# An expert gets 112 slots in place of 128, and the overflow pass three blocks in place of two

## The reference

```
s    = sigmoid(h @ router_w);  sb = s + router_b            # 16 experts in 4 groups
grp  = group with the largest sum of its two best sb
eidx = the two best experts inside grp;  w = s[eidx] / sum(s[eidx])
for e in 16 experts:
    a = silu(h @ w_g[e]) * (h @ w_u[e])                       # 1024 -> 512
    y = y + gates[:, e] * (a @ w_d[e])                        # 512 -> 1024
x = x + gate2 * y
```

## Time and profile before

| | |
|---|---|
| timed runs, us | 1648.64, 1649.46, 1653.35 |
| profiled execution, from first to last instruction | 1646.0 us (3.5 under the median; the profile gives no other time of its own) |
| TensorE busy, multiplications | 1567.6 us, 95%, 7693 |
| VectorE, ScalarE, GpSimd busy | 64%, 56%, 32% |
| moved by DMA | 381.8 MB, mean 232 GB/s |
| granted TensorE clock, mean | 0.984 |

### The profile page before, as it was taken

The page is one execution under the profiler, slowest core; times in us unless marked ns, Lnnn a source line. Parts: engine busy times, 40 slices in busy tenths (PEclk is TensorE's granted clock), DMA queues, the critical chain, the costliest instruction groups (busy, mean ns, idle before and its releaser), DMA issues.

```text
span 1646.0 us, 21287 instructions
## 1 busy us (share of the span) xinstructions
PE 1567.6 (95%) x7693; PEld 1234.8 (75%) x7693; DVE 1047.2 (64%) x1385; ACT 923.8 (56%) x1284; POOL 530.5 (32%) x271
## 2 busy tenths in 40 slices
PE   7999999989999999999889999999999989999996
PEld 4677778877775887888676777787767778888885
DVE  2226546673355898998862357377433479899998
ACT  3343445434335788888644343444353458888893
POOL 2344554444532111111234445444445131111112
PEclk9999999999998999999999999999999999999998
DMA  9765343344359999999946543422443469999995
GB/s 363 265 199 167 115 128 91 102 130 143 115 174 334 344 385 362 370 377 364 368 170 210 187 154 112 133 90 89 144 147 111 157 224 379 378 368 378 381 368 205
DMA packets 153822, 381.77 MB, mean 232 GB/s; under 512 B 21060, under 2 KB 26886, under 8 KB 153724
## 3 DMA queue, kind: packets, MB, share of 16 engines
q1 hardware_dynamic: 122704, 325.32, 56.2%
q10 hardware_dynamic: 20140, 36.56, 6.3%
q0 software_dynamic: 10880, 18.59, 3.1%
HBM read 378.55 MB, written 27.93 MB: 247 GB/s over the span
## 4 chain that ended last, share of the span: by engine, by line
PE 70%; DVE 12%; DMA 10%; ACT 5%; issue 2%; ACTq 0%; SPq 0%; POOL 0%; DVEq 0%; POOLq 0%
PE ps L606 56%; PE ps L615 4%; DVE wxl L2466 4%; DMA raw<-w_e_down 4%; DMA raw<-w_e_up 3%; PE ps L639 2%; PE ps L952 2%; ACT wxh L1826 1%; DMA own<-w_mod 1%; PE ps L980 1%; PE ps L886 1%; DVE uv L2241 1%; ACT wh L1331 1%; PE ps L658 1%; PE ps L650 1%
## 5 line engine op out<-in xcount | busy, mean ns | idle before, releaser
L1949 POOL TENSOR_TENSOR wl<-raw,wh 128x1024 fp32r<-128x1024 f32 x168 | 409.8, 2443 | 531.7 <-ACT wh L1331 531.5
L2466 DVE TENSOR_TENSOR wxl<-raw,wxh 128x1024 fp32r<-128x1024 f32 x384 | 454.5, 1220 | 55.2 <-ACT wxh L1826 52.5
L1826 ACT ACTIVATE wxh<-raw 128x1024 fp32r<-128x1024 f32 x384 | 402.6, 1061 | 92.4 <-DMA raw<-w_e_down 35.4
L606 PE MATMUL ps<-wxh,xeT 128*128 128x512 f32 x1024 | 341.3, 399 | 4.0 <-issue 2.5
L1331 ACT ACTIVATE wh<-raw 128x1024 fp32r<-128x1024 f32 x168 | 176.7, 1056 | 227.6 <-PE ps L606 223.2
L606 PE MATMUL ps<-wh,hTh 128*128 128x512 f32 x720 | 293.2, 407 | 5.9 <-DVE hTl L2088 3.3
L606 PE MATMUL ps<-wh,hTl 128*128 128x512 f32 x720 | 281.9, 392 | 0.0
L606 PE MATMUL ps<-wl,hTh 128*128 128x512 f32 x720 | 281.5, 391 | 0.0
L606 PEld LDWEIGHTS ps<-wxh,xeT 128*128 128x128 f32 x1024 | 193.3, 189 | 46.8 <-issue 4.3
L606 PE MATMUL ps<-wxl,xeT 128*128 128x512 f32 x512 | 199.9, 390 | 0.0
L606 PEld LDWEIGHTS ps<-wh,hTh 128*128 128x128 f32 x720 | 135.7, 188 | 40.7 <-issue 7.9
(11 more groups left out here) (282 smaller groups left out, 2177.3 us busy)
## 6 DMA issues: line engine op xcount, KB each, us to landing
raw<-w_e_gate SPq DMA_DIRECT2D x128, 512.0 KB, 6.5
raw<-w_e_up SPq DMA_DIRECT2D x128, 512.0 KB, 5.8
raw<-w_e_down SPq DMA_DIRECT2D x128, 512.0 KB, 5.5
raw<-w_in SPq DMA_DIRECT2D x120, 512.0 KB, 3.7
own<-w_mod ACTq DMA_DIRECT2D x27, 1024.0 KB, 7.6
raw<-w_mod SPq DMA_DIRECT2D x36, 512.0 KB, 5.1
raw<-w_br_b SPq DMA_DIRECT2D x16, 512.0 KB, 3.8
raw<-w_out SPq DMA_DIRECT2D x16, 512.0 KB, 3.8
```

What stands on the lines that cost most here:

```text
L606: ins = pe.matmul(out, act_hl[i], w_hl[j], start=start and n == 0, stop=stop and n == 2)
L1826: act.activation(wxh[:, q % RING_MOE, :, :], raw[:, place, :, :], ACT.Copy).then_inc(sem("hi_done"), 1)
L1949: pool.tensor_tensor(wl[:, p % RING, :, :], raw[:, PAIR_CHUNK[p] % RAW, :, :], wh[:, p % RING, :, :].bitcast(F32), ALU.subtract).then_inc( ...
L2466: dve.tensor_tensor(wxl[:, q % RING_MOE, :, :], raw[:, expert_chunk(l, 0, q)[0], :, :], wxh[:, q % RING_MOE, :, :].bitcast(F32), ALU.subtr ...
```

## The change

The number of slots per expert becomes `SLOTS = 112`. All tiles keep their size; each instruction that handles an expert's slots takes 112 of the 128 partitions (where slots lie on partitions) or 112 of each 128 columns (where they lie in the free dimension). The overflow pass starts at rank 112 and has three blocks of 128 ranks in place of two, so its body is longer by a third block on every engine. Outside that body the instructions of each engine and their order are the same as before.

```diff
+SLOTS = 112
+BLOCKS_OVER = -(-(T - SLOTS) // P)
 def second_pass(eng, l, turn):
-                for b in (1, 2):
+                for b in range(1, BLOCKS_OVER + 1):
                     turn(e, b)
...
 # tensor_program
 def turn_rows(k, half, bank):
-    last = transpose(ps[:, bank, i * P:(i + 1) * P], xg[:, k % 2, first:first + 2 * P - 1:2])
+    last = transpose(ps[:, bank, i * P:i * P + SLOTS], xg[0:SLOTS, k % 2, first:first + 2 * P - 1:2])
 def up_pair(e, q, k, i):
-    last = mm3(ps[:, 2 + i // 4, :], (xeT[:, k % 2, 0, j, :], xeT[:, k % 2, 1, j, :]),
+    last = mm3(ps[0:SLOTS, 2 + i // 4, :], (xeT[:, k % 2, 0, j, 0:SLOTS], xeT[:, k % 2, 1, j, 0:SLOTS]),
 def down_pair(e, q, i):
-    last = mm3(ps[:, bank, :], (src[:, 0, j, :], src[:, 1, j, :]),
+    last = mm3(ps[0:SLOTS, bank, :], (src[:, 0, j, 0:SLOTS], src[:, 1, j, 0:SLOTS]),
 def turn_act(count):
-    last = transpose(ps[:, 0, j * P:(j + 1) * P], ae[:, j * P:(j + 1) * P])
+    last = transpose(ps[:, 0, j * P:j * P + SLOTS], ae[0:SLOTS, j * P:(j + 1) * P])
...
 # scalar_program
 def gate_part(count, pair):
-    act.activation(sg[:, :], ps[:, 2, :], ACT.Silu)
+    act.activation(sg[0:SLOTS, :], ps[0:SLOTS, 2, :], ACT.Silu)
 def rows_hi(count, k):
-    act.activation(xeT[:, k % 2, 0, :, :], ps[:, 0:2, :].rearrange("p b (k n) -> p (b k) n", n=P), ACT.Copy
+    act.activation(xeT[:, k % 2, 0, :, 0:SLOTS], ps[:, 0:2, :].rearrange("p b (k n) -> p (b k) n", n=P)[:, :, 0:SLOTS], ACT.Copy
...
 # gpsimd_program
-    pool.indirect_dma_start(xg[:, k % 2, :], None, h2_rows[:, :],
+    pool.indirect_dma_start(xg[0:SLOTS, k % 2, :], None, h2_rows[:, :],
...
 # vector_program
-dve.tensor_scalar(flag[:, 0:1], cnt[:, 0:1], float(P - SLOT_BASE), None, ALU.is_gt)
+dve.tensor_scalar(flag[:, 0:1], cnt[:, 0:1], float(SLOTS - SLOT_BASE), None, ALU.is_gt)
 def rows_lo(e, k, count):
-    dve.tensor_tensor(xeT[:, k % 2, 1, :, :], ps[:, 0:2, :].rearrange("p b (k n) -> p (b k) n", n=P),
-                      xeT[:, k % 2, 0, :, :].bitcast(F32), ALU.subtract)
+    dve.tensor_tensor(xeT[:, k % 2, 1, :, 0:SLOTS], ps[:, 0:2, :].rearrange("p b (k n) -> p (b k) n", n=P)[:, :, 0:SLOTS],
+                      xeT[:, k % 2, 0, :, 0:SLOTS].bitcast(F32), ALU.subtract)
 def turn(e, b):
-    dve.tensor_scalar(cnt[:, 2:5], slot[...], float(-P * b), None, ALU.add)
+    dve.tensor_scalar(cnt[:, 2:5], slot[...], float(-(SLOTS + P * (b - 1))), None, ALU.add)
```

More of the change, by code:

```diff
@@ L1158, in token_sums @@
                 for t in range(NT):
-                    last = pe.matmul(out, pick[:, k % 2, t, :], tokens_r[:, t, :], start=t == 0, stop=t == NT - 1)
+                    last = pe.matmul(out, pick[:, k % 2, t, 0:SLOTS], tokens_r[:, t, :], start=t == 0, stop=t == NT - 1)
                 last.then_inc(sem("idx_acc"), 1)
@@ L1315, in tensor_program @@
                     for s in range(2):
-                        last = pe.matmul(ps[:, LAST_BANKS[u], :], pickT[:, odd, t, :], oes[odd][:, s, half * W:(half + 1) * W],
+                        last = pe.matmul(ps[:, LAST_BANKS[u], :], pickT[0:SLOTS, odd, t, :], oes[odd][0:SLOTS, s, half * W:(half + 1) * W],
                                          start=odd == 0 and s == 0, stop=odd == 1 and s == 1)
@@ L1843, in act_hi @@
                 act.wait_ge(sem("eT_acc"), at("eT_acc", l, 1) + count)
-                act.activation(dst[:, 0, :, :], ps[:, 0, :].rearrange("p (k n) -> p k n", k=4), ACT.Copy
+                act.activation(dst[:, 0, :, 0:SLOTS], ps[:, 0, :].rearrange("p (k n) -> p k n", k=4)[:, :, 0:SLOTS], ACT.Copy
                                ).then_inc(sem("eT_hi"), 1)
@@ L1852, in out_row @@
                     act.wait_ge(sem(name), (e - k % 2) * 8 + at(name, l, 0))
-                act.activation(oe_rows[k % 2][:, :].rearrange("p (b n) -> p b n", b=2), ps[:, 4:6, :], ACT.Identity,
-                               scale=slot_gate[:, k % 4:k % 4 + 1]).then_inc(sem("out_hi"), 1)
+                act.activation(oe_rows[k % 2][0:SLOTS, :].rearrange("p (b n) -> p b n", b=2), ps[0:SLOTS, 4:6, :], ACT.Identity,
+                               scale=slot_gate[0:SLOTS, k % 4:k % 4 + 1]).then_inc(sem("out_hi"), 1)
             def out_hi(k, pair):
@@ L1859, in out_hi @@
                 act.wait_ge(sem("scattered0"), at("scattered0", l, 16 * LOOSE // 2))
-                act.activation(oes[k % 2][:, 0, :].rearrange("p (b n) -> p b n", b=2), ps[:, 4:6, :], ACT.Identity,
-                               scale=slot_gate[:, k % 4:k % 4 + 1]).then_inc(sem("out_hi"), 1)
+                act.activation(oes[k % 2][0:SLOTS, 0, :].rearrange("p (b n) -> p b n", b=2), ps[0:SLOTS, 4:6, :], ACT.Identity,
+                               scale=slot_gate[0:SLOTS, k % 4:k % 4 + 1]).then_inc(sem("out_hi"), 1)
             def expert(e, k):
@@ L1889, in scalar_program @@
                 act.wait_ge(sem("X_acc"), at("X_acc", l, 1 + half))
-                act.activation(xeT[:, 0, 0, 4 * half:4 * half + 4, :], ps[:, 3 + half, :].rearrange("p (k n) -> p k n", k=4), ACT.Copy
+                act.activation(xeT[:, 0, 0, 4 * half:4 * half + 4, 0:SLOTS],
+                               ps[:, 3 + half, :].rearrange("p (k n) -> p k n", k=4)[:, :, 0:SLOTS], ACT.Copy
                                ).then_inc(sem("xe_hi"), 1)
@@ L1908, in scalar_program @@
                 act.wait_ge(sem("pair_used"), used_at(l, NE - 1, HEAD + 1 + 2 * half))
-                act.activation(oes[1][:, 0, half * W:(half + 1) * W], ps[:, 6 + half, :], ACT.Identity,
-                               scale=slot_gate[:, k:k + 1]).then_inc(sem("out_hi"), 1)
+                act.activation(oes[1][0:SLOTS, 0, half * W:(half + 1) * W], ps[0:SLOTS, 6 + half, :], ACT.Identity,
+                               scale=slot_gate[0:SLOTS, k:k + 1]).then_inc(sem("out_hi"), 1)
             def turn(e, b):
@@ L2554, in vector_program @@
             make_pick(1, 1)
-            slot_rows(0, 0, ps[:, 6, 0:2])
-            slot_rows(1, 1, ps[:, 7, 0:2])
+            slot_rows(0, 0, ps[0:SLOTS, 6, 0:2])
+            slot_rows(1, 1, ps[0:SLOTS, 7, 0:2])
             make_pick(2, 2)
```

64 lines of the change are left out of this document (32 added, 32 removed).

## The result

The changed kernel is slower: median 1662.92 us of five runs (1659.38 to 1666.56) against 1649.38 of five runs of the kernel before on the same chip (1646.95 to 1653.35), ratio 1.0075 with an interval of 1.0057 to 1.0094 (the quotient of the two medians alone is 1.0082). The forecast was 1647.3, range 1639 to 1654: 2.2 us faster, which a measurement could not have told from no change. The profiled execution of the changed kernel spans 1661.1 us, 15.1 more than before. The same windows as in the earlier trace rows show where: fourteen experts of layer 0, of layer 1, then three single experts (length, then busy time and count of PE, PEld, DVE, ACT and POOL, granted clock, DMA share, GB/s).

What follows compares the result with a forecast made beforehand. TensorE's stream was taken as the bound, with the weights' arrival (DMA share 0.99) close beside it. Transposes -1.7, evictions -0.5 and layer ends -0.5 sum to -2.7, counted as -2.2: 1647.3 us, range 1639 to 1654.

Steps and rivals of the forecast that it cites:

- Step (5): Gather and scatter of an expert's rows: naming 112 rows changes nothing, as unused slots were skipped and GpSimd has free time.
- first rival: Expert multiplications: part of 0.227 us pays for stationary columns, so 112 saves time, capped by supply at 6 to 9 us; 0.2.
- Step (1): The 2304 expert multiplications: 112 stationary columns leave the 0.227 us distance, set by 512 moving columns; 0, bound -31 us.
- slower rival's partial form: Expert multiplications: the 112-column load partly fails to go ahead, 4 to 8 ns each, +9 to +18 us.
- Step (2): The 384 transposes: the activations' get shorter with 112 moving columns, -1.7 us; the gathered rows' stay, 0.
- Steps (3) and (4): Evictions on ScalarE and VectorE shorten: -0.5 us in supply-bound experts, and -0.5 at the first and last experts of layers.
- second pass: Overflow pass: runs if an expert has over 112 rows, 0.8 ms a layer; chance 0.01.
- faster rival: Expert multiplications: the load is in the 0.227 us and 112 columns give time back, about 1641 us; chance 0.2.
- slower rival: Expert multiplications: the 112-column load doesn't go ahead of the running one, +207 us in full; 0.03 in full.
- in part or by stalls that fall worse: Expert loops: a partly delayed weight load or worse supply stalls give 1651 to 1670 us; chance 0.11.
- ScalarE's waits for DMA beyond 34 us in 240: Expert loops: a sign against the forecast, to be checked if multiplications stood 0.225 us or less apart.
- DMA share unchanged: Expert loops: a sign that the forecast was right, the DMA engines' share staying at the 0.99 of before.

Runs made afterwards that it cites:

- e2: The changed kernel with its expert multiplications and the splits that feed them back at 128 columns; 1663.16 us, ratio 1.0080 to the kernel before.
- e6: The changed kernel with gather and its picks, multiplications and splits back at 128; 1648.26 us, ratio 0.9987 to the kernel before.
- e1: The kernel before with only its expert multiplications at 112 stationary columns; 1648.45 us, ratio 0.9997.
- e5: The changed kernel with only the gather and the picks that feed it back at 128 rows; 1645.89 us, ratio 0.9985 to the kernel before.
- e10: The kernel before with gathers and scatters of 64 rows, unfetched rows cleared by GpSimd, tokens beyond rank 63 left out; 1656.41 us, ratio 1.0043.
- e3: The kernel before with only a third block added to the overflow pass that isn't entered; 1644.55 us, ratio 0.9966.

## Why the prediction was wrong, by its steps

**Step (5), the row transfers, failed.** It read: "The gather and scatter name 112 rows; unused slots were skipped already. GpSimd is busy 35.3 us of 252, so its time is free." It priced the step at the engine that issues it and at the rows that move, and both prices were nothing. The resource that the rows use is the DMA engines, whose share I had read as 0.99 and called one of the two things that bound the stage. I let its time per packet stand as it was, and gave it no bounds, though the trace had no indirect gather of other than 128 rows. What the runs showed in its place: 6.7 us more for the same weight packets and 1.9 more for the rows in layer 0's loop (q1 and q0 above), and 14 to 15 us in all between e2 and e6. The 6 to 9 us of room under TensorE that the first rival worked out was used up, and the supply set the end: the waits for split weights show it (3.6 us against 0.2), and so does the chain. An unused slot wasn't free either. Queue 0 of the whole run has 9920 packets now and had 10880: 16 slots for each of 60 transfers, so a skipped slot still moves one small packet, of 4 bytes and 9 ns on the mean. 960 x 9 / 16 is 0.5 us gained. The page's line on HBM counts such a slot as if its row had moved: read 378.55 and 376.39 MB before and after, a difference of 512 rows of 4224 bytes, which queue 0 never carried (18.59 MB in both).

**Step (1), the multiplications**, took 0 and was mis-sized. The distance went from 227 to 231 ns, the foot of the 4 to 8 ns of the slower rival's partial form, which I priced at 9 to 18 us. e1 has it alone and shows nothing in the timed runs: the shortest expert grew by 0.14 us and not by 72 x 0.004 = 0.29, since the median distance isn't everyone's (the mean of the unbroken ones went from 227.8 to 230.5), and the loops by 1.9 and 2.2, which is 14 x 0.14. At 120 columns the shortest expert grew by 0.39 and the loops by 3.6 and 3.9, less than 14 x 0.39 = 5.5: an expert that waits for weights anyway takes in part of it. The argument that nothing hangs on the load was right in one way: the load measures 177 ns as worked out, and a shorter load bought nothing. By the rule weighed in the prediction (the Trainium skill, TensorE: Matmul & The Clock Gate, Weight-path perf modes — Fast Weight Load (FWL) and DoubleRow), losing the 128-column form should lengthen a load that had it; here it became shorter, 189 to 177 ns, in line with 163 at 96 columns. But a width was a risk with a sign that the trace of before couldn't give, and it isn't in order of width: 227, 234, 231, 230 ns at 128, 120, 112, 96 (at 112 the median is 229 to 231, by kernel and layer: 229 in e5). Its cause is open.

**Step (2), the transposes.** The row transposes stayed at 0.86, as forecast. The activation's went from 0.354 to 0.317 (medians of the loops) and not to 0.30: 32 x 0.037 is 1.2 of the 1.7 us.

**Steps (3) and (4), the evictions.** All four sizes came out: 900 and 532 on ScalarE, 1080 and 617 on VectorE. What they were worth can be bounded by e5, which has all the savings and no slow gather, against e6, which has only the transposes' and partitions' share: 1645.89 and 1648.26, no difference that this measurement tells (and e5 carries the longer distance of the multiplications). The sum of -2.2 is neither shown nor refuted: e5, which is the change with a whole gather, is 3.4 us under the kernel before by the medians, and its interval takes in no change.

**The rivals.** The second pass was not entered: TensorE has 7693 matrix instructions in both. The faster rival falls: 112 columns gave nothing back. The slower rival had the right side and the wrong mechanism; a stream that costs 4 ns more is there, but e2, without it, is as slow. Its range for "in part or by stalls that fall worse", 1651 to 1670 at a chance of 0.11, held the measured 1662.9; as no step of it named the transfers, that was luck. What I said would prove me wrong in the profile, ScalarE's waits for DMA beyond 34 us in 240, came (44.0), though I had tied it to a faster TensorE. And "DMA share unchanged" was no test at all: a share of 0.99 can't show that each packet takes longer. The rate does, 364 against 372 GB/s.

**Why a gather of fewer rows is slower is not shown.** The trace has no record of which DMA engine wrote which partition. The Trainium skill (DMA: Bandwidth & Descriptors, The descriptor swizzle) says that in a transfer to 128 partitions each of the 16 engines writes only one port of the memory; if fewer rows are dealt out to the engines in another way, they would cross ports with each other and with the weights. That would fit what is slow (all counts but 128, the rows themselves and their neighbours, and only while many rows move), but no run here shows the deal. e10 speaks against its simplest form: dealt out as 4 each, 64 rows would again start at a multiple of four partitions on every engine, and their packets were the slowest. A gather of 128 rows beside a scatter of fewer was run (e5, e6), and a slow scatter was not seen in any run; a gather of fewer rows with its packets on other partitions wasn't tried.

## What to carry to other kernels

Where the DMA share stands at 0.99, price every transfer that a change touches in the DMA engines' time, packets times ns of one, with bounds on the ns, and not only in bytes or in the time of the engine that issues it. Where such a gather runs beside a full stream of weights, try it at 128 rows with the unused ones skipped, even if fewer are needed: the skipped rows cost 9 ns each spread over 16 engines, the shorter gather cost 14 to 16 us here. Look at GB/s and at time per packet beside the share, which can't rise any more, and count the slow packets, since the median of 159 ns showed nothing. And before a difference of a few us is put down to a change, see what two builds of the same instructions differ by (6 us here).

## What the runs showed of the hardware

- An indirect gather from DRAM of 64, 96, 112 or 120 rows, in the loops: 195 to 232 ns on the mean for a packet of 4224 bytes, against 164 to 168 with 128 rows. Weight packets beside the row transfers 181 to 192 ns against 165 to 171. An indirect scatter of 64 to 120 rows: no difference (159 to 160 ns for a packet of 4096 bytes).
- The means move by a part of the packets: in the changed kernel 28% of the weight packets beside row transfers took 170 to 400 ns (1.6% before), and gathers of 8 to 12 rows kept 164 ns.
- Weight packets are *quicker* on the mean beside a 128-row gather or scatter (165 ns) than away from one (175). The medians are equal (159); packets over 400 ns are rarer there (0.7% against 2.3%).
- A slot skipped as out of range: a packet of its own, of 4 bytes and about 9 ns.
- The distance of two 512-column float32r multiplications by stationary columns: 227 (128), 234 (120), 229 to 231 (112), 230 ns (96), while the load shortens from 189 to 177.
- Two builds with the same executed instructions differ by 6 us in 1650 (e3, 0.9966).
